# One chunk first, modulation chunks moved back, and a norm's residual scaling spread out

## The chip, the cores and the metric

The kernel runs on one core of one Trainium2 chip. The metric is the device time of one execution in microseconds (us); the kernel before took 3770.34 us (median of three runs, 3767.11 to 3773.52).

## The reference, cut to what matters

A first block of two layers (each: feed-forward, token mixer, feed-forward, all with modulation and a post-norm) is followed by a second block of two layers with RMS norms. The change touches the first block only. Activations are 512 tokens by 1024 features.

```python
cond = silu(c)
for l in range(2):
    mod = cond @ w_ada[l] + b_ada[l]                 # 1024 x 9216, then split into nine parts of 1024
    sh1, sc1, g1, sh2, sc2, g2, sh3, sc3, g3 = split(mod, 9)
    y = swiglu(x * (1 + sc1) + sh1, w_gate, w_up, w_down)     # 1024 -> 2816 -> 1024
    x = layer_norm(ALPHA * x + 0.5 * (1 + g1) * y)
    y = token_mixer(x * (1 + sc2) + sh2, w_in, w_out)
    x = layer_norm(ALPHA * x + (1 + g2) * y)
    y = swiglu(x * (1 + sc3) + sh3, ...)
    x = layer_norm(ALPHA * x + 0.5 * (1 + g3) * y)
```

## The kernel before, in words

**Layout.** Everything is transposed: a tile is 128 features by 512 tokens, and the residual XR is eight such tiles (`NT` = 8). Products are taken in three matmuls on a high and a low part of both operands (`mul3`: high by high, high by low, low by high). HH and HL are the two parts of a stage's input h, WH and WL those of a weight chunk, AH and AL those of the feed-forward's hidden tiles.

**Weight stream.** Weights come in chunks of 256 output columns (128 x 2048 floats, 1 MB). SyncE issues each as one DMA into one of three staging buffers (STAGE, `NS` = 3), in the order in which the plan takes the chunks. `split` lets ScalarE copy a chunk into one of two WH buffers (`NW` = 2) once the chunk that held the buffer is done, and `low` lets VectorE subtract to get WL; TensorE waits for that ("w.lo"). A staging buffer is free for the chunk three places on when WL is there. `take` gives out the next chunk, and splits the one after it first; `ahead`, called inside a norm, does that a little earlier for the second chunk of the coming stage, but only if the place right behind the first chunk in the stream is a weight chunk: a raw chunk there makes it return nothing.

**Modulation.** The matrix w_ada has 72 chunks. Eight are done at the start; the other 64 are raw chunks, strung into the same stream. `take` adds `rate` (0.62) to `due` for most chunks, and when `due` reaches 1 it calls `ada`, which puts one modulation chunk right behind the chunk just taken: nine VectorE operations (`ada_rows`, L1892 to L1898). After every second one, `ada_flush` follows two releases later: TensorE sums over partitions (`ada_sum`, eight matmul instructions) and VectorE adds the bias. `modded` flushes at once if a pending pair holds values that the caller needs. `ffn` calls it for its gate through `gate`, right after the first tile of the first down chunk.

**Start of a stage.** `ffn` and `first_mixer` begin with `pair`: three dummy matmuls (`keep`), then for the first chunk the products with h tiles 0 to 2 (18 matmuls), the same for the second chunk, then tile 3 of both, then the rest of the first and the rest of the second: 96 matmuls. `pair` is there because h comes tile by tile. In the stream it takes the chunk `self.taken`, so a modulation chunk between the two is simply passed.

**Norm.** `layer_norm` plans `ln_a` (mean, subtraction, squares, variance), `ln_b` (scale, and h tile by tile on VectorE, ScalarE and GpSimd) and `ln_x`, eight ScalarE operations on the residual (L1627), which are planned right behind h and ahead of the next stage's first `take`.

**Background.** `tick` is called after each few matmuls in the plan and advances the generators in `self.active` by one step each; attention units are run that way. Each engine's program is the plan's steps in order; engines meet at semaphores only.

Of the kernel before, what the change touches and what calls it, by code (L numbers as in the profile page):

```python
# [22 lines left out]
ACT = mybir.ActivationFunctionType  # L23
# [5 lines left out]
NT = D // P  # L29
# [9 lines left out]
FFN_GROUPS = [(0, 8), (8, 8), (16, 6)]  # L39
ODD_ORDER = (4, 5, 0, 6, 1, 7, 2, 3)  # L40
MLP_GROUPS = [(0, 8), (8, 8), (16, 8), (24, 8)]
# [57 lines left out]
class Plan:  # L99
# [241 lines left out]
    def layer_norm(self, l, idx, total, nxt):  # L341
        sid, acc = total
        if nxt:
            self.modded(nxt[0], nxt[2])
            self.modded(nxt[0], nxt[1])
        s, mean = self.small.take(), self.banks.take()
        self.tmp.free(acc[0], ("ln.mean", sid))
        sq = []
        for n in range(NT):
            sq.append(self.tmp.take())  # L350
            if n in (1, 3, 5):
                self.tmp.free(sq[n - 1], ("ln.fold", sid, n))
        self.tmp.free(sq[6], ("ln.fold", sid, 7))
        var = self.held.take()
        low = self.ahead()
        self.add("ln_a", l, idx, sid, acc[0], nxt, list(self.xv), s, mean, sq, var, low)
        self.banks.free(mean, ("ln.sub", sid, NT - 1))
        for n in (1, 3, 5, 7):
            self.tmp.free(sq[n], ("ln.var", sid, n))
        y, rs = self.yr.take(), self.banks.take()  # L360
        self.held.free(var, ("rs.v", sid))
        if nxt:
            self.hv += 1
            self.add("ln_b", sid, y, var, rs, s, self.hfree, self.hv, self.to_h(), low)
            self.banks.free(rs, ("ln.sc", sid, NT - 1))
            self.add("ln_x", sid, s, self.hv, [v + 1 for v in self.xv])
            self.xv = [v + 1 for v in self.xv]
            self.small.free(s, ("x", NT - 1, self.xv[NT - 1]))
            self.yr.free(y, ("ln.rs", sid))
            return None  # L370
        sq = []
        for n in range(NT):
            sq.append(self.tmp.take())
            if n in (1, 2, 3, 5):
                self.tmp.free(sq[n - 1], ("ll.fold", sid, n))
        self.tmp.free(sq[6], ("ll.fold", sid, 7))
        self.xv = [v + 1 for v in self.xv]
        self.add("ln_last", l, idx, sid, y, var, rs, sq, list(self.xv), low)
        self.banks.free(rs, ("ll.x", sid, NT - 1))
        self.yr.free(y, ("ln.rs", sid))  # L380
        self.small.free(s, ("ln.sub", sid, NT - 1))
        return [(sq[n], ("ll.fold", sid, n)) for n in (3, 5, 7)]

    def rms_norm(self, name, l, total, meanwhile=None):
        rid, low = self.new(), None
# [18 lines left out]
            meanwhile[1]()  # L404


    def ffn(self, kind, st, names, l, groups, gate, mean):
        total = (self.new(), [])
        afree = [None, None]
        for gi, (g0, G) in enumerate(groups):  # L410
            self.av += 1
            av, a = self.av, gi % 2
            for mi in range(G // 2):
                idx, first = l * names["n_up"] + g0 // 2 + mi, gi == 0 and mi == 0
                qs = []
                ch = self.take(names["gate" if kind == "swiglu" else "up"], idx)
                for t, (b, pid) in enumerate(self.pair(ch, "h", self.hv) if first else self.feat2(ch, 8, "h", self.hv)):
                    q = self.tmp.take()
                    self.add("act", kind, pid, b, q)
                    self.banks.free(b, ("act", pid))  # L420
                    if kind == "swiglu":
                        qs.append((q, pid))
                    else:
                        self.add("a_part", av, a, 2 * mi + t, q, ("act.sq", pid), afree[a])
                        self.tmp.free(q, ("a.lo", av, 2 * mi + t))
                self.release(ch, ("proj", pid))
                if kind == "swiglu":
                    ch = self.take(names["up"], idx)
                    for t, (b, pid) in enumerate(self.feat2(ch, 8, "h", self.hv)):
                        q, gid = qs[t]  # L430
                        self.add("glu", pid, gid, b, q)
                        self.banks.free(b, ("glu", pid))
                        self.add("a_part", av, a, 2 * mi + t, q, ("glu", pid), afree[a])
                        self.tmp.free(q, ("a.lo", av, 2 * mi + t))
                    self.release(ch, ("proj", pid))
            if gi == len(groups) - 1:
                self.hfree = ("proj", pid)
            done, s = [], None
            for c in range(4):
                ch = self.take(names["down"][gi], l * 4 + c, ada=gi < len(groups) - 1 or c == 0)  # L440
                for t in range(2):
                    b, pid = self.feat(ch, G, 256, t, "a%d" % a, av)
                    if gate and not gate[-1]:
                        gate[-1] = self.gate(l, gate[0], 0.5)
                    self.upd(2 * c + t, b, pid, gate[-1] if gate else None)
                    done.append(2 * c + t)
                self.release(ch, ("proj", pid))
                afree[a] = ("proj", pid)
                if gi == len(groups) - 1 and mean:
                    self.total(mean, *total, done[:-2] if c < 3 else done)  # L450
                    done = done[-2:] if c < 3 else []
        if gate:
            self.small.free(gate[-1][0], ("x", NT - 1, self.xv[NT - 1]))
        return total if mean != "rms" else self.squares(*total)
# [41 lines left out]
    def first_mixer(self, l):  # L496
        hv = self.hv
# [2 lines left out]
        nk_done, sb_done, out_done = {}, [], {}  # L500

        def proj(idx, key, paired=False):
            ch = self.take("w_in", l * 12 + idx)
            for t, (b, pid) in enumerate(self.pair(ch, "h", hv) if paired else self.feat2(ch, 8, "h", hv)):
                self.add("m_copy", l, key, t, pid, b)
                self.banks.free(b, ("m.p", l, key, t))
            self.release(ch, ("proj", pid))
# [129 lines left out]
        for c in range(2):  # L637
            ch = self.take("w_in", l * 12 + 4 + c)
# [16 lines left out]
        gate = self.gate(l, 5, 1.0)  # L655
# [482 lines left out]
    def whole(self):  # L1138
        self.ada_first()
        self.fill = [(0, c) for c in range(8, 36)] + [(1, c) for c in range(36)]  # L1140
        self.modulate_first()
        ffn1 = {"gate": "ffn1_w_gate", "up": "ffn1_w_up", "down": ["ffn1_down0", "ffn1_down1", "ffn1_down2"], "n_up": 11}
        ffn2 = {"gate": "ffn2_w_gate", "up": "ffn2_w_up", "down": ["ffn2_down0", "ffn2_down1", "ffn2_down2"], "n_up": 11}
        for l in range(2):
            self.rate = 0.62
            total = self.ffn("swiglu", "f1%d" % l, ffn1, l, FFN_GROUPS, [2, None], "ln")
            self.layer_norm(l, 0, total, (l, 3, 4))
            total = self.first_mixer(l)
            self.layer_norm(l, 1, total, (l, 6, 7))
            if l == 1:  # L1150
                self.add("c2_load", self.hv)
                self.bg.append(self.rope_tables())
            total = self.ffn("swiglu", "f2%d" % l, ffn2, l, FFN_GROUPS, [8, None], "ln")
            total = self.layer_norm(l, 2, total, (1, 0, 1) if l == 0 else None)
        assert not self.fill
        self.pipeline()
        mlp = {"up": "w_up", "down": ["down_m0", "down_m1", "down_m2", "down_m3"], "n_up": 16}
        for l in range(2):
            self.rms_norm("g_mix", l, total)
            if l == 0:  # L1160
                self.even_mixer()
            else:
                self.odd_mixer()
            total = self.cross(l, ("w_out_e", "w_out_o")[l])
            self.rms_norm("g_mlp", l, total)
            total = self.ffn("relu2", "mlp%d" % l, mlp, l, MLP_GROUPS, None, "rms" if l == 0 else None)
        self.add("store", list(self.xv))


# [397 lines left out]
def scalar(e, m, plan):  # L1567
# [52 lines left out]
                act.activation(m.HH[:, n, :], m.XR[:, n, :], ACT.Identity, bias=B[:, n:n + 1], scale=A[:, n:n + 1]).then_inc(  # L1620
                    *e.up("act_hh", "h.hi", hv, n))

    def ln_x(sid, s, hv, xv):
        AG, AB = m.small(s)[:, 16:24], m.small(s)[:, 24:32]
        for n in range(NT):
            e.wait_ge(("h.hi", hv, n), ("h.q", hv, n))
            act.activation(m.XR[:, n, :], m.XR[:, n, :], ACT.Identity, bias=AB[:, n:n + 1], scale=AG[:, n:n + 1]).then_inc(  # L1627
                *e.up("act_x", "x", n, xv[n]))

    def ln_last(l, idx, sid, y, var, rs, sq, xv, low_of):  # L1630
        beta = m.vec("ln_bias", l * 24 + idx * 8, 8)
# [1273 lines left out]
```

## Time and profile before

| | |
|---|---|
| median of the timed runs | 3770.34 us (3767.11 to 3773.52) |
| profiled execution, its own time | 3772.04 us |
| its span in the trace | 3770.7 us |
| TensorE matmuls | 3610.5 us busy, 96% of the span |
| VectorE / ScalarE / GpSimd | 1765.6 / 1234.9 / 497.4 us |
| chain that ended last | 85% matmuls of L1236 |

The matmul line of nearly all projections is L1236, so a tile's name tells them apart: `s_hh,s_wh` is h by a chunk's high part, `s_cc` alone is a dummy matmul, `s_cc,s_tmp` with one column is a sum over partitions. A row of the timeline has start, length, engine, line, operation, and in brackets how long the engine had been idle and what it waited for. Matmuls overlap, so the distance of two starts is the rate, not the length of one.

### The profile page before, as it was taken

To read this page: it belongs to the slowest core of one execution; us is meant where nothing else is said; L and a number is where in the kernel's file an instruction comes from. 1 tells how busy PE (TensorE), PEld (TensorE's weight loads), DVE (VectorE), ACT (ScalarE), POOL (GpSimd) and SP (SyncE) were. 2 spreads that over 40 slices of the span, in tenths; PEclk is the share of its full clock that TensorE was granted. 3 is DMA by queue.
4 is the path that set the end of the run, shared out by engine and by line. 5 is a ranking of instruction groups with operands and counts; after the bars stand their busy time and mean duration, and the time that the engine had idled before them with its cause. 6 is when DMAs were issued, how large, how long until landed. Compare 5 with 4: busy or idle time off the path is not lost.

```text
span 3770.7 us, 41104 instructions
## 1 busy us (share of the span) xinstructions
PE 3610.5 (96%) x16878; PEld 2921.0 (77%) x16878; DVE 1765.6 (47%) x3091; ACT 1234.9 (33%) x1670; POOL 497.4 (13%) x433
## 2 busy tenths in 40 slices
PE   8999999999998999999999999988999999999999
PEld 7888867688886888867788877746878887787888
DVE  4444553554545444444532244785553334554332
ACT  2222361342223222462332223335442223343222
POOL 0010110110011010121110010111121111202111
PEclk9999999999998999999999998978999999999999
DMA  6444222134442434211122221101212222222222
GB/s 243 159 147 152 104 90 90 56 123 145 158 144 82 164 145 145 90 45 45 56 99 92 98 84 56 57 12 34 90 67 90 101 101 81 90 79 78 101 92 76
DMA packets 52605, 373.42 MB, mean 99 GB/s; under 512 B 5825, under 2 KB 5953, under 8 KB 9538
## 3 DMA queue, kind: packets, MB, share of 16 engines
q1 hardware_dynamic: 52418, 370.79, 27.4%
q8 instruction: 133, 2.18, 0.2%
q14 instruction: 54, 0.44, 0.0%
HBM read 368.67 MB, written 2.10 MB: 98 GB/s over the span
## 4 chain that ended last, share of the span: by engine, by line
PE 85%; DVE 8%; ACT 4%; issue 2%; POOL 1%; DMA 0%; DVEq 0%; ACTq 0%; SPq 0%; POOLq 0%
PE ps L1236 85%; DVE s_wl L1879 1%; ACT s_wh L1571 1%; PE ps L1261 0%; DVE s_tmp L2109 0%; ACT L1676 0%; ACT s_tmp L1707 0%; DVE s_hl L1872 0%; DVE s_tmp L2099 0%; POOL s_tmp L2385 0%; DVE s_xr L1959 0%; ACT s_hh L1571 0%; DVE s_tmp L2015 0%; DVE s_sm L2107 0%; DVE s_na L1862 0%
## 5 line engine op out<-in xcount | busy, mean ns | idle before, releaser
L1236 PE MATMUL ps<-s_hh,s_wh 128*128 128x512 f32 (+1 forms) x2840 | 1133.2, 399 | 56.3 <-DVE s_wl L1879 31.5
L1236 PE MATMUL ps<-s_hl,s_wh 128*128 128x512 f32 (+1 forms) x2840 | 1115.0, 393 | 0.0
L1236 PE MATMUL ps<-s_hh,s_wl 128*128 128x512 f32 (+1 forms) x2840 | 1113.6, 392 | 0.0
L1879 DVE TENSOR_TENSOR s_wl<-s_stage,s_wh 128x2048 fp32r<-128x2048 f32 (+3 forms) x296 | 634.7, 2146 | 744.5 <-ACT s_wh L1571 744.4
L1571 ACT ACTIVATE s_wh<-s_stage 128x2048 fp32r<-128x2048 f32 (+1 forms) x277 | 519.9, 1877 | 771.6 <-PE ps L1236 661.1
L1236 PEld LDWEIGHTS ps<-s_hh,s_wh 128*128 128x128 f32 (+1 forms) x2840 | 538.3, 190 | 202.0 <-issue 41.4
L1236 PEld LDWEIGHTS ps<-s_hh,s_wl 128*128 128x128 f32 (+1 forms) x2840 | 537.5, 189 | 115.6
L1236 PEld LDWEIGHTS ps<-s_hl,s_wh 128*128 128x128 f32 (+1 forms) x2840 | 538.3, 190 | 111.3 <-issue 2.2
L1236 PE MATMUL ps<-s_ah,s_wh 128*128 128x512 f32 x1216 | 475.6, 391 | 0.0
L1236 PE MATMUL ps<-s_ah,s_wl 128*128 128x512 f32 x1216 | 474.3, 390 | 0.0
L1236 PE MATMUL ps<-s_al,s_wh 128*128 128x512 f32 x1216 | 474.1, 390 | 0.0
L2405 POOL TENSOR_TENSOR s_al<-s_tmp,s_ah 128x512 fp32r<-128x512 f32 x152 | 196.4, 1294 | 1749.2 <-ACT s_ah L1571 1749.2
L1236 PEld LDWEIGHTS ps<-s_ah,s_wl 128*128 128x128 f32 x1216 | 228.7, 188 | 47.8
L1236 PEld LDWEIGHTS ps<-s_al,s_wh 128*128 128x128 f32 x1216 | 228.9, 188 | 47.0
L1236 PEld LDWEIGHTS ps<-s_ah,s_wh 128*128 128x128 f32 x1216 | 228.8, 188 | 47.1
L1595 ACT ACTIVATE s_tmp<-ps 128x512 f32<-128x512 f32 x152 | 90.8, 597 | 498.4 <-PE ps L1236 498.1
L1571 ACT ACTIVATE s_ah<-s_tmp 128x512 fp32r<-128x512 f32 x152 | 96.0, 632 | 417.1 <-DVE s_tmp L2030 361.9
L1930 DVE SCALAR_TENSOR_TENSOR s_xr<-ps,s_sm,s_xr 128x512 f32<-128x512 f32 x112 | 83.6, 749 | 225.1 <-PE ps L1236 224.5
L1932 DVE TENSOR_TENSOR s_xr<-ps,s_xr 128x512 f32<-128x512 f32 x96 | 66.2, 690 | 232.6 <-PE ps L1236 232.6
L1895 DVE SCALAR_TENSOR_TENSOR s_tmp<-s_stage,s_cond,s_tmp 128x256 f32<-128x256 f32 x366 | 150.8, 478 | 0.0
L2030 DVE TENSOR_TENSOR s_tmp<-s_tmp,ps 128x512 f32<-128x512 f32 x88 | 60.2, 686 | 168.5 <-PE ps L1236 168.3
L1236 PEld LDWEIGHTS ps<-s_cc,s_tmp 128*128 128x128 f32 x852 | 115.2, 209 | 22.2 <-POOL s_tmp L2396 6.7
(416 smaller groups left out, 3445.5 us busy)
## 6 DMA issues: line engine op xcount, KB each, us to landing
s_stage<-in_w_ada SPq DMA_DIRECT2D x64, 1024.0 KB, 4.8
s_stage<-in_ffn_w_gate SPq DMA_DIRECT2D x44, 1024.0 KB, 4.8
s_stage<-in_ffn_w_up SPq DMA_DIRECT2D x44, 1024.0 KB, 4.8
s_stage<-in_ffn_down SPq DMA_DIRECT2D x32, 1024.0 KB, 4.8
s_stage<-in_w_up SPq DMA_DIRECT2D x32, 1024.0 KB, 4.7
s_stage<-in_down_m SPq DMA_DIRECT2D x32, 1024.0 KB, 4.8
s_stage<-in_w_in SPq DMA_DIRECT2D x24, 1024.0 KB, 4.8
s_stage<-in_ffn_down SPq DMA_DIRECT2D x16, 768.0 KB, 4.2
```

Source lines behind the costliest of these rows:

```text
L1236: return pe.matmul(out, lhs, rhs, start=start, stop=stop, skip_group_check=True)
L1571: return act.activation(out, src, ACT.Copy)
L1595: act.activation(m.tmp(q), m.bank(b), ACT.Silu if kind == "swiglu" else ACT.Relu).then_inc(*e.up("act_ffn", "act", pid))
L1879: ins = dve.tensor_tensor(m.WL[:, ws, a:z], m.STAGE[:, j % NS, a:z], m.WH[:, ws, a:z].bitcast(F32), ALU.subtract)
L1895: ins = dve.scalar_tensor_tensor(dst, w[:, k, :], cond, dst, ALU.mult, ALU.add)
L1930: ins = dve.scalar_tensor_tensor(x, m.bank(b), m.small(gate[0])[:, n:n + 1], x, ALU.mult, ALU.add)
L1932: ins = dve.tensor_tensor(x, m.bank(b), x, ALU.add)
L2030: dve.tensor_tensor(m.tmp(q), m.tmp(q), m.bank(b), ALU.mult).then_inc(*e.up("dve_ffn", "glu", pid))
L2405: pool.tensor_tensor(m.AL[a][:, k, :], m.tmp(q), m.AH[a][:, k, :].bitcast(F32), ALU.subtract).then_inc(*e.up("pool_a", "a.lo", av, k))
```

## The change

The first feed-forward of layer 0 no longer begins with `pair`; its first chunk runs alone, both tiles in step with h, without dummy matmuls. The first chunk (mixer) or the first two (feed-forward) of a stage no longer add to `due`. `rate` is 0.64 in place of 0.62. `ln_x` does one tile per call, and the calls are made by a generator that `tick` advances: two ticks do nothing, then one tile per tick. An argument of `ffn` that nothing used is gone.

```diff
@@ layer_norm
-            self.add("ln_x", sid, s, self.hv, [v + 1 for v in self.xv])
             self.xv = [v + 1 for v in self.xv]
-            self.small.free(s, ("x", NT - 1, self.xv[NT - 1]))
+            self.active.append(self.scaled(sid, s, self.hv, list(self.xv)))
...
+    def scaled(self, sid, s, hv, xv):
+        yield
+        for n in range(NT):
+            yield
+            self.add("ln_x", sid, s, hv, n, xv[n])
+        self.small.free(s, ("x", NT - 1, xv[NT - 1]))
@@ ffn
-    def ffn(self, kind, st, names, l, groups, gate, mean):
+    def ffn(self, kind, names, l, groups, gate, mean, paired=True):
...
-                ch = self.take(names["gate" if kind == "swiglu" else "up"], idx)
-                for t, (b, pid) in enumerate(self.pair(ch, "h", self.hv) if first else self.feat2(ch, 8, "h", self.hv)):
+                ch = self.take(names["gate" if kind == "swiglu" else "up"], idx, ada=not first)
+                both = first and paired
+                tiles = self.pair(ch, "h", self.hv) if both else self.feat2(ch, 8, "h", self.hv, first)
+                for t, (b, pid) in enumerate(tiles):
...
-                    ch = self.take(names["up"], idx)
+                    ch = self.take(names["up"], idx, ada=not first)
@@ first_mixer, proj
-            ch = self.take("w_in", l * 12 + idx)
+            ch = self.take("w_in", l * 12 + idx, ada=not paired)
@@ whole
-            self.rate = 0.62
-            total = self.ffn("swiglu", "f1%d" % l, ffn1, l, FFN_GROUPS, [2, None], "ln")
+            self.rate = 0.64
+            total = self.ffn("swiglu", ffn1, l, FFN_GROUPS, [2, None], "ln", l > 0)
@@ scalar
-    def ln_x(sid, s, hv, xv):
+    def ln_x(sid, s, hv, n, v):
         AG, AB = m.small(s)[:, 16:24], m.small(s)[:, 24:32]
-        for n in range(NT):
-            e.wait_ge(("h.hi", hv, n), ("h.q", hv, n))
-            act.activation(m.XR[:, n, :], ...).then_inc(*e.up("act_x", "x", n, xv[n]))
+        e.wait_ge(("h.hi", hv, n), ("h.q", hv, n))
+        act.activation(m.XR[:, n, :], ...).then_inc(*e.up("act_x", "x", n, v))
```

## Rows read from the trace of the kernel before

**Rows 1.** The page, part 1: busy time, share of the span, instructions.
```profile
PE 3610.5 (96%) x16878; PEld 2921.0 (77%) x16878; DVE 1765.6 (47%) x3091; ACT 1234.9 (33%) x1670; POOL 497.4 (13%) x433
```

**Rows 2.** Waits of TensorE: who waited for whom, total us, times, longest.
```profile
PE ps L1236 <- DVE s_wl L1879: 33.9, 7, 13.9
```

**Rows 3.** The chain that ended last, in time: start, length, what.
```profile
54.20 369.26 PE ps L1236 x1644
...
1173.52 2.30 DVE s_wl L1879
1175.86 368.27 PE ps L1236 x1644
```

**Rows 4.** Timeline of TensorE, the first feed-forward's start.
```profile
39.83 2.93 PE L1236 MATMUL ps<-s_cc 128*128 128x256 f32 x6 [2.45 <-DVE s_wl L1879]
42.20 0.99 PE L1236 MATMUL ps<-s_hh,s_wh 128*128 128x512 f32 x1
54.20 0.79 PE L1236 MATMUL ps<-s_hh,s_wh 128*128 128x512 f32 x1 [7.06 <-DVE s_wl L1879]
60.28 0.40 PE L1236 MATMUL ps<-s_hh,s_wl 128*128 128x512 f32 x1
74.84 0.39 PE L1236 MATMUL ps<-s_hh,s_wh 128*128 128x512 f32 x1
```

**Rows 5.** Windows: bounds, length, matmul busy (count), granted clock, DMA share, GB/s.
```profile
54.20:60.21 6.01, 6.01 (x14) 0.50 0.50 174
```

**Rows 6.** Timeline of ScalarE and VectorE in the same stretch.
```profile
49.92 1.89 ACT L1571 ACTIVATE s_wh<-s_stage 128x2048 fp32r<-128x2048 f32 x1
49.46 0.69 DVE L1872 TENSOR_TENSOR s_hl<-s_tmp,s_hh 128x512 fp32r<-128x512 f32 x1
51.85 2.29 DVE L1879 TENSOR_TENSOR s_wl<-s_stage,s_wh 128x2048 fp32r<-128x2048 f32 x1 [1.70 <-ACT s_wh L1571]
```

**Rows 7.** Windows around a TensorE pause of 4.81 us that ended at 3170.29.
```profile
3166.30:3169.75 3.45, 0.00 (x0) 1.00 0.00 0
3169.75:3173.17 3.42, 2.88 (x7) 0.50 0.55 172
```

**Rows 8.** Timeline of the stage start at 1156 us: TensorE, then ScalarE.
```profile
1156.52 0.51 PE L1236 MATMUL ps<-s_hh,s_wh 128*128 128x512 f32 x1 [0.24 <-DVE s_hl L1872]
1195.30 0.39 PE L1236 MATMUL ps<-s_hh,s_wl 128*128 128x512 f32 x1
1165.95 5.73 ACT L1627 ACTIVATE s_xr<-s_xr,s_sm 128x512 f32<-128x512 f32 x8
1189.60 1.28 ACT L1595 ACTIVATE s_tmp<-ps 128x512 f32<-128x512 f32 x2 [16.12 <-PE ps L1236]
```

**Rows 9.** Timeline of TensorE, first and 96th matmul of the stage at 1558 us.
```profile
1558.70 0.50 PE L1236 MATMUL ps<-s_hh,s_wh 128*128 128x512 f32 x1
1581.38 0.39 PE L1236 MATMUL ps<-s_hh,s_wl 128*128 128x512 f32 x1
```

**Rows 10.** Timeline of TensorE, VectorE and GpSimd at the first down chunk.
```profile
141.08 0.95 PE L1236 MATMUL ps<-s_cc,s_tmp 128*128 128x1 f32 x8
149.70 0.42 DVE L1898 TENSOR_TENSOR s_tmp<-s_tmp 128x256 f32<-128x256 f32 x1
142.71 1.30 POOL L2405 TENSOR_TENSOR s_al<-s_tmp,s_ah 128x512 fp32r<-128x512 f32 x1 [4.16 <-ACT s_ah L1571]
```

**Rows 11.** Timeline of VectorE: modulation chunk and attention step in mixer 0; a chunk's low part in mixer 1.
```profile
496.71 0.42 DVE L1898 TENSOR_TENSOR s_tmp<-s_tmp 128x256 f32<-128x256 f32 x1
497.05 0.74 DVE L2053 TENSOR_TENSOR s_tmp<-s_tmp,ps 128x256 f32<-128x256 f32 x2
...
1584.24 2.29 DVE L1879 TENSOR_TENSOR s_wl<-s_stage,s_wh 128x2048 fp32r<-128x2048 f32 x1 [3.15 <-ACT s_wh L1571]
```

**Rows 12.** Windows: both mixers, from first h matmul to the next stage's.
```profile
439.75:769.35 329.60, 309.10 (x1566) 0.95 0.21 77
1558.70:1874.75 316.05, 301.26 (x1535) 0.96 0.15 54
```

More of the change, by code:

```diff
@@ L1152, in whole @@
                 self.bg.append(self.rope_tables())
-            total = self.ffn("swiglu", "f2%d" % l, ffn2, l, FFN_GROUPS, [8, None], "ln")
+            total = self.ffn("swiglu", ffn2, l, FFN_GROUPS, [8, None], "ln")
             total = self.layer_norm(l, 2, total, (1, 0, 1) if l == 0 else None)
@@ L1165, in whole @@
             self.rms_norm("g_mlp", l, total)
-            total = self.ffn("relu2", "mlp%d" % l, mlp, l, MLP_GROUPS, None, "rms" if l == 0 else None)
+            total = self.ffn("relu2", mlp, l, MLP_GROUPS, None, "rms" if l == 0 else None)
         self.add("store", list(self.xv))
@@ L1621, in ln_b @@
                     *e.up("act_hh", "h.hi", hv, n))
-    def ln_x(sid, s, hv, xv):
+    def ln_x(sid, s, hv, n, v):
         AG, AB = m.small(s)[:, 16:24], m.small(s)[:, 24:32]
-        for n in range(NT):
-            e.wait_ge(("h.hi", hv, n), ("h.q", hv, n))
-            act.activation(m.XR[:, n, :], m.XR[:, n, :], ACT.Identity, bias=AB[:, n:n + 1], scale=AG[:, n:n + 1]).then_inc(
-                *e.up("act_x", "x", n, xv[n]))
+        e.wait_ge(("h.hi", hv, n), ("h.q", hv, n))
+        act.activation(m.XR[:, n, :], m.XR[:, n, :], ACT.Identity, bias=AB[:, n:n + 1], scale=AG[:, n:n + 1]).then_inc(
+            *e.up("act_x", "x", n, v))
     def ln_last(l, idx, sid, y, var, rs, sq, xv, low_of):
```

## The prediction

> **What bounds the kernel now.** I read the page's busy table first: TensorE's matmuls fill 96% of the span, and VectorE, the next engine, less than half [rows 1]. So time can come only from stretches in which TensorE stands still or runs slowly. TensorE's waits name the largest of them: VectorE's low part of a weight chunk (L1879), 33.9 us in 7 waits, one of 13.9 us [rows 2]. The chain in order of time shows where: a feed-forward is a run of 368 us or so with nothing else in it, and the run that starts at 1175.86 comes directly after a low part at 1173.52 [rows 3]. Inside feed-forwards nothing waits; at their starts something does. The timeline gives the two places: a 7.06 us wait that ends at 54.20 [rows 4] and the 13.9 us one. The granted clock adds a second price, for after the 7.06 us wait TensorE has 0.50 of its clock (1.2 GHz) for 6.01 us [rows 5]. Fourteen matmuls take 60.28 - 54.20 = 6.08 us there, 0.434 us each, and the next 64 take 74.84 - 60.28 = 14.56 us, 0.2275 each [rows 4].
>
> **Part 1, the first feed-forward begins with one chunk.** Before: 18 matmuls from 42.20, then the wait for the second chunk's low part (ScalarE's copy at 49.92, VectorE's 2.29 us to 54.14 [rows 6]), then the other 78 of the pair's 96, so that the third chunk begins at 74.84 [rows 4]. Now the first chunk has all 48 of its matmuls to do before it needs the second. Tile 7 of h is ready at 50.15 [rows 6], tiles come about 1.2 us apart and six matmuls take 6 x 0.2275 = 1.37, so h does not hold them up. The plan still puts the second chunk's copy behind the same sixteen ScalarE operations, so 54.14 stays.
> The three dummy matmuls go too (six instructions, 39.83 to 42.76 [rows 4]). They were hidden, as TensorE had nothing else to do, but they had TensorE streaming when h came. Without them it has done only one-column sums and then paused. I take it to begin at 0.50: if low for t us, it falls back by t/2. t is between the 3.4 us of the short low stretch in [rows 7] and the 6.0 us of [rows 5]; I take 4.5, nearer to the start's own 39.83 to about 43, where it rose. 96 matmuls from 42.20 then end at 42.20 + 96 x 0.2275 + 2.25 = 66.3. The second chunk is asked for at 42.20 + 10.92 + 2.25 = 55.4, after 54.14, so there is no wait. Gain 74.84 - 66.3 = **8.5 us** (bounds 7.8 and 9.1).
> The rule that speaks against this edit is in the Trainium skill (TensorE: Matmul & The Clock Gate, section "What's actually happening"): the throttled clock is the default and activity releases it, so leaving out warming work means a cold start. No row shows this start without the dummies. By that rule the sum stands as above. If the clock were up within a microsecond as before, the first chunk would end near 53.5, wait for 54.14, and the gain would be about 9.7.
> The third chunk needs the first one's buffer: free at 55.4, then two evictions of 0.64 each [rows 8], a copy of 1.9 and a low part of 2.3 [rows 6] make it ready at about 60.9, before 66.3.
>
> **Part 2, no modulation chunk among the first two.** I counted `due` through the whole plan. With 0.62 a modulation chunk comes in a stage's first two only once, at the second layer's first feed-forward, between gate and up. There `ahead` finds a raw chunk and returns nothing; the up chunk's copy then stands behind the eight ScalarE operations of L1627 (1165.95, 5.73 us [rows 8]). First matmul to 96th is 1195.30 - 1156.52 = 38.78 us [rows 8]. At the stage start at 1558.70, where `ahead` works, it is 1581.38 - 1558.70 = 22.68 [rows 9]; the three other stages with the pair's second chunk ready also take 22.7. The norm ahead is no longer for it. Gain 38.78 - 22.68 = **16.1 us**; this contains the slow clock after the wait. It has a near-exact twin, so I give it only 1 us either way.
> The same count moves the others. In the first feed-forward modulation chunks 8, 9, 10 now stand behind up 1, up 2 and gate 3, and chunk 11, which stood behind gate 3, now stands behind the **first down chunk**. The gate needs exactly chunks 8 to 11 and is planned after that chunk's first tile: the flush puts a sum on TensorE that waits for chunk 11's nine VectorE operations. This is a wait that was not there. Its price: chunk 12 stands in that place now and ends at 149.70 + 0.42 = 150.12. The sum before it at 141.08 goes, so the first tile's 24 matmuls run from 141.08 to 146.54 (the last hidden tile, at 144.01, is in time [rows 10]), and TensorE stands until 150.2: 3.7 us. The sum itself is only moved. Behind it are queued the down chunk's second tile on TensorE and, on VectorE, the bias, the gate, both residual updates and the next low part, which has a chunk's length in hand. To this comes the clock: after a pause of 4.81 us it was at 0.50 for 3.42 us, 2.88 of them busy, 1.44 lost [rows 7]. I take 1.4: **+5.1 us** (bounds 0, if chunk 11 is done early, and 3.7 + 3.0, if the clock is low for the 6.0 us of [rows 5]).
>
> **Part 3, rate and the mixers.** The number of modulation chunks is 64 as before. Mixer 0 keeps eight, two of them moved by one or two chunks; mixer 1 gets its first, chunk 71, behind its second weight chunk. There VectorE is idle 3.15 us after one low part [rows 11], and one chunk takes some 3.4, so nearly all is hidden; the sum of its pair on TensorE (0.95 us [rows 10]) moves there from a feed-forward and is no gain or loss. A modulation chunk between a low part and an attention step's subtraction, as that ending at 497.05 [rows 11], does delay the step by its 3.4 us. With eight of them mixer 0 takes 329.60 against 316.05, 13.55 or 1.7 each [rows 12]. I take +0.5 for the one more (bounds -2, if one leaves the chain of steps, and +3.4).
>
> **Part 4, the residual's scaling spread out.** Forty operations as before, none added; only their place on ScalarE changes: four ahead of the first chunk's evictions, four behind. Ahead of the first eviction ScalarE is idle 16.12 us [rows 8], which hides all eight either way, and their first reader is the residual update at the stage's end. **0**; if that cover were gone, 5.73 us at each of five norms. Where it did matter, at 1166, part 2 already counts it.
>
> **Sum.** -8.5 - 16.1 + 5.1 + 0.5 = -19.0 us. On the profiled execution: 3772.04 - 19.0 = 3753.0. That execution is 1.7 above the median of 3770.34, so I forecast **3751.3 us**.
>
> **Rivals.** *The new sum does not wait* (TensorE is slower to it, or chunk 11 is done by then): -24.1, 3746. For it: bounds of zero; against: the same VectorE order at 149.70 now. *The start gains nothing*, because h or the cold clock stretches the first chunk, or the third chunk comes late: -10.5, 3760. *The wait at 1162 stays in part*: the up chunk's copy is freed of the 5.73 us but is not made ahead: -8.5 - 5.7 + 5.6 = -8.6, 3762. *The order is not what I counted* and both waits stay: within 0.2%, 3770. **Slower**: the spread operations stand ahead of something TensorE waits for. In five norms 8 x 0.72 = 5.73 us each is 28.7; with -19.0 it gives +9.7, 3780. It turns the sign once over 19.0 / 5 = 3.8 us per norm is exposed, and against it stand the idle 16.12 us, and that ScalarE is busy for 33% only [rows 1].
>
> **How the numbers follow.** Forecast 0.55, no wait 0.15, start gains nothing 0.11, wait stays in part 0.09, order not as counted 0.04, slower 0.06. Bounds of the parts around the forecast: 3745 to 3757. To leave out no more than two in ten, and since three runs of the kernel before already spread over 6 us, the range is 3744 to 3760. Changes under 0.2% (7.5 us) cannot be told from none; all cases but the last two are beyond that, though the two small ones only just: faster 0.90, same 0.05, slower 0.05.
>
> **What would show it.** In the changed profile: 48 matmuls without a wait from about 42, the first ones 0.43 us apart, and the third chunk begun near 66; no L1879 wait near 1145, and 22.7 us from first to 96th matmul there; a new TensorE wait of 3 to 4 us for a sum near 138 us, behind the first 24 matmuls on hidden tiles; the mixers within 2 us of 329.6 and 316; L1627 in single operations. Wrong would be a wait for L1879 in either start, more than 3 us more in mixer 1, or ScalarE named by TensorE's waits after a norm.

## The result, and the profile after

Times in us: median, lowest and highest of the single runs.

| | before | changed |
|---|---|---|
| median | 3770.52 (12 runs) | 3761.68 (12 runs, 3758.06 to 3771.74) |
| ratio | | 0.9981, 95% interval 0.9972 to 0.999 |
| profiled execution, its span | 3772.04, 3770.7 | 3758.06, 3756.7 |
| mean granted clock in it | 0.966 | 0.969 |

The ratio is not the quotient of the medians: it lies near that of the means (3762.95 and 3770.12), and so reads 7.2 us where the medians differ by 8.8. The same holds for the tables below.

By the medians the changed kernel is 8.8 us faster where I had forecast 19.0, and 3761.7 lies outside my range of 3744 to 3760. The profiled executions alone differ by 14.0: that of before lay 1.5 above its median, that of the changed kernel 3.6 below its own. So 5.0 of the missing 10.2 can be looked for in the profile, and the other 5.1 or so are these two distances.

The busy table of the changed kernel, to be laid beside [rows 1]:
```profile
PE 3609.8 (96%) x16872; PEld 2917.7 (78%) x16872; DVE 1765.9 (47%) x3093; ACT 1235.4 (33%) x1670; POOL 497.4 (13%) x433
```
Six dummy matmuls are gone, and TensorE's busy time is within 0.7 us of before. The gain is in its waits (who waited for whom, total, times, longest; L1887 is the low part, L1906 the end of a modulation chunk, L2425 the rope product on GpSimd):
```profile
PE ps L1245 <- DVE s_wl L1887: 11.2, 6, 4.8
PE ps L1245 <- POOL s_nk L2425: 10.4, 6, 4.1
```
Against [rows 2] the wait for low parts fell from 33.9 to 11.2 us. The second line, which the text below calls the wait for the rope product, rose from 7.7 us in 6 waits, the longest 3.5 (in the kernel before it is `PE ps L1236 <- POOL s_nk L2417`).

**The start.** TensorE's timeline there, beside [rows 4]:
```profile
42.07 0.77 PE L1245 MATMUL ps<-s_hh,s_wh 128*128 128x512 f32 x1 [4.82 <-POOL s_hl L2369]
42.64 0.63 PE L1245 MATMUL ps<-s_hl,s_wh 128*128 128x512 f32 x1
...
46.90 0.44 PE L1245 MATMUL ps<-s_hh,s_wl 128*128 128x512 f32 x1
...
66.27 0.39 PE L1245 MATMUL ps<-s_hh,s_wh 128*128 128x512 f32 x1
```
The first matmuls are 0.43 us apart and last 0.63, until about 46.9; from there on they are 0.2275 apart and last 0.39. The third chunk begins at 66.27 (74.84 before), and no wait for a low part stands between. The windows view (bounds, length, busy time and count of matmuls, weight loads, VectorE, ScalarE and GpSimd, then granted clock, DMA share, GB/s) reads a granted clock of 1.00 from 42.07 to 46.90, so its records miss this stretch, and only the spacing and length of the matmuls show that the engine was at the lower of its two levels (1.2 GHz):
```profile
42.07:46.90 4.83, 4.83 (x11) 3.77 (x12) 4.83 (x7) 4.83 (x8) 3.20 (x2) 1.00 0.51 213
```
The Trainium skill (TensorE: Matmul & The Clock Gate, section "What's actually happening") has the throttled clock as the default that activity releases; the trace agrees, with 4.8 us in which matmuls start half as often as behind it.

**The norm at 1158**, beside [rows 8], TensorE and then ScalarE:
```profile
1158.18 0.79 PE L1245 MATMUL ps<-s_hh,s_wh 128*128 128x512 f32 x1
1180.89 0.39 PE L1245 MATMUL ps<-s_hh,s_wl 128*128 128x512 f32 x1
```
```profile
1167.62 2.92 ACT L1635 ACTIVATE s_xr<-s_xr,s_sm 128x512 f32<-128x512 f32 x4
1175.20 1.28 ACT L1604 ACTIVATE s_tmp<-ps 128x512 f32<-128x512 f32 x2 [4.66 <-PE ps L1245]
```
First to 96th matmul is 22.71 us in place of 38.78. Four of the eight scalings (L1635) now stand ahead of the first eviction, the rest behind it; TensorE names none of them.

**The gate's sum.** TensorE at the first down chunk, beside [rows 10], and the windows around the new wait, with the columns as above:
```profile
141.64 1.02 PE L1245 MATMUL ps<-s_cc,s_tmp 128*128 128x1 f32 x8 [3.54 <-DVE s_tmp L1906]
```
```profile
138.10:141.64 3.54, 0.00 (x0) 0.03 (x1) 3.41 (x10) 0.00 (x0) 0.00 (x0) 1.00 0.64 222
141.64:146.00 4.36, 4.36 (x16) 3.67 (x17) 1.09 (x3) 0.00 (x0) 0.00 (x0) 0.61 0.77 301
```
TensorE has nothing for 3.54 us while VectorE works through the nine operations of modulation chunk 11, and then has matmuls 0.43 us apart, half clock, until about 146.0. From the first down chunk's first matmul to that of the next chunk on h it takes 49.81 us in place of 44.61, that is +5.20.

**The mixers**, beside [rows 12], with the columns as above:
```profile
436.34:771.37 335.03, 312.94 (x1566) 237.69 (x1567) 166.72 (x334) 139.62 (x218) 50.75 (x58) 0.94 0.21 76
1545.92:1861.39 315.47, 300.73 (x1543) 229.34 (x1543) 143.09 (x268) 139.59 (x218) 50.72 (x58) 0.97 0.16 57
```
Mixer 0 takes 5.4 us more, mixer 1 takes 0.6 less. The stretches of the program add up to the difference of -14.0. The start, up to the first down chunk, has -9.3: 8.4 of them come before the third chunk, and 0.8 is a modulation sum that no longer stands there. The gate has +5.2. Mixer 0 with its norm and the next feed-forward up to its first down chunk has +4.5. The norm at 1158, counted up to the next down chunk, has -16.2, and the norm ahead of mixer 1 +1.6. The rest moves by 1 us or less each.

### The profile page after: what moved, and what is told of

The parts are those of the page before. It is cut to its first block, busy times and chain, and to the rows that moved or that the text cites. A ratio compares the mean times of both kernels' runs of the same rounds, so it can differ in the third digit from the quotient of the medians.

```text
span 3756.7 us, 41109 instructions
## 1 busy us (share of the span) xinstructions
PE 3609.8 (96%) x16872; PEld 2917.7 (78%) x16872; DVE 1765.9 (47%) x3093; ACT 1235.4 (33%) x1670; POOL 497.4 (13%) x433
## 4 chain that ended last, share of the span: by engine, by line
PE 86%; DVE 7%; ACT 4%; issue 2%; POOL 1%; DMA 0%; DVEq 0%; SPq 0%; ACTq 0%; POOLq 0%
PE ps L1245 86%; DVE s_wl L1887 1%; ACT s_wh L1580 1%; PE ps L1270 0%; ACT L1684 0%; POOL s_tmp L2393 0%; DVE s_tmp L2117 0%; ACT s_tmp L1715 0%; DVE s_tmp L2107 0%; DVE s_tmp L2023 0%; DVE s_hl L1880 0%; ACT s_hh L1580 0%; DVE s_tmp L1903 0%; POOL s_hl L2369 0%; DVE s_sm L2115 0%
## 5 line engine op out<-in xcount | busy, mean ns | idle before, releaser
L1887 DVE TENSOR_TENSOR s_wl<-s_stage,s_wh 128x2048 fp32r<-128x2048 f32 (+3 forms) x298 | 634.5, 2132 | 704.1 <-ACT s_wh L1580 704.0
L2034 DVE TENSOR_TENSOR s_tmp<-s_tmp 128x512 f32<-128x512 f32 x64 | 47.1, 736 | 166.7 <-ACT s_tmp L1604 166.5
```

Of the source, the lines that this page charges most:

```text
L1887: ins = dve.tensor_tensor(m.WL[:, ws, a:z], m.STAGE[:, j % NS, a:z], m.WH[:, ws, a:z].bitcast(F32), ALU.subtract)
L2034: dve.tensor_tensor(m.tmp(q), m.tmp(q), m.tmp(q), ALU.mult).then_inc(*e.up("dve_ffn", "act.sq", pid))
```

## The experiments

Here "the chunks' order" is the list of weight chunks behind which the plan puts a modulation chunk. In most of these kernels it is written out, as a set AT of indices (counted from 0 over the whole program), and the rate no longer matters:

```
-        self.due += self.rate if ada else 0
-        if self.due >= 1:
-            self.due -= 1
+        self.taken_w += 1
+        if self.taken_w - 1 in AT:
             ...
```
The kernel before ran again beside each four of them: its median was 3770.44 for e1 to e4, 3770.33 for e5 to e8 and 3772.08 for e9 to e12. Differences are of medians, against that value.

### The changed kernel once more, and its three parts alone

e1 is the changed kernel unchanged. e2 has the start alone:
```
-  def ffn(self, kind, st, names, l, groups, gate, mean):
+  def ffn(self, kind, st, names, l, groups, gate, mean, paired=True):
...
-  self.pair(ch, "h", self.hv) if first else self.feat2(ch, 8, "h", self.hv)
+  self.pair(ch, "h", self.hv) if first and paired else self.feat2(ch, 8, "h", self.hv, first)
...
-  total = self.ffn("swiglu", "f1%d" % l, ffn1, l, FFN_GROUPS, [2, None], "ln")
+  total = self.ffn("swiglu", "f1%d" % l, ffn1, l, FFN_GROUPS, [2, None], "ln", l > 0)
```
e3 has the order alone:
```
-  ch = self.take(names["up"], idx)            (and the same for gate)
+  ch = self.take(names["up"], idx, ada=not first)
...
-  ch = self.take("w_in", l * 12 + idx)
+  ch = self.take("w_in", l * 12 + idx, ada=not paired)
...
-  self.rate = 0.62
+  self.rate = 0.64
```
e4 has the scaling alone:
```
-  self.add("ln_x", sid, s, self.hv, [v + 1 for v in self.xv])
+  self.active.append(self.scaled(sid, s, self.hv, list(self.xv)))
...                                             (`scaled` and `ln_x` as in the change)
```

> The changed kernel once more. Its first profile is 14.0 us shorter than the profile of before, its median 8.8. Theory A (the schedule made mixer 0 longer): the profile again shows 334 to 336 us from mixer 0's first h matmul to the next stage's, against 329.6 before, and the 3.5 us wait for the modulation sum at the first down chunk; the gains at the start (8.5) and at the layer 1 norm (16.2) are there too. Theory B (chance of the clock): mixer 0 comes out within 1.5 us of 329.6 in this profile, because its low stretches fall elsewhere. Both expect a spread of single times of more than 6 us.

> The kernel before with only the first feed-forward begun by one chunk; modulation chunks and the residual's scaling as before. All theories: TensorE's 7.06 us wait gone, the third chunk begun 8.5 us earlier, no wait for a modulation sum near 141, the norm at 1156 still with its 13.9 us wait. 8.5 us shorter than before (7.8 to 9.1 by the clock's start), 3762. If leaving out the dummy matmuls costs more than I took, 4 to 6 us shorter only.

> The kernel before with only the modulation chunks moved (none among a feed-forward's first two, rate 0.64); the pair and the scaling as before. Theory A1 (the moved modulation chunks lengthen mixer 0): -16.1 at the norm, +5.1 for the sum at the first down chunk, +5 in mixer 0: 6 us shorter, 3764.5, and mixer 0 at 334 to 336. Theory A2 (the spread scaling lengthens it) and B (clock): 11 us shorter, 3759.5, mixer 0 within 1.5 us of 329.6.

> The kernel before with only the residual's scaling spread out. Theory A2 (ScalarE's spread operations stand in mixer 0's attention steps): mixer 0 at 334 to 336, but at the layer 1 norm the up chunk's copy no longer stands behind 5.7 us of them, so in sum about 1 us shorter, 3769. Theory A1 and B: mixer 0 unchanged, and up to 5.7 us saved at that norm: 3765. My prediction's part 4 said 0 with the order changed.

| | median (runs) | ratio, 95% interval | difference |
|---|---|---|---|
| e1, changed again | 3759.25 (8) | 0.9975, 0.9965 to 0.9984 | -11.2 |
| e2, start alone | 3762.45 (9) | 0.9982, 0.9972 to 0.9992 | -8.0 |
| e3, order alone | 3771.01 (12) | 1.0003, 0.9995 to 1.0011 | +0.6 |
| e4, scaling alone | 3769.76 (11) | 0.9998, 0.999 to 1.0007 | -0.7 |

The three add up to -8.1, and the changed kernel has -8.8 or -11.2. So by the medians the start gives all of the gain, and the order, from which I had expected -10.5 (-16.1 + 5.1 + 0.5), gives nothing, although its profile shows the norm's gain in full (from the norm's first matmul to the next down projection 89.97 us, 106.19 before) and the gate's +5.2. Something else in the order must cost about what the forecast is short of. e4 shows by the way that the spread scaling alone frees the up chunk's copy (that same stretch is 4.7 us shorter), but its median does not tell this from no change.

e1's profile, which spans 3756.0 us, repeats the start, the gate's +5.2 and the norm at 1158. In the mixers it differs: mixer 0 takes 330.99 us, 1.4 more than before where the first profile had 5.4, and mixer 1 takes 319.87, 3.8 more where the first had 0.6 less. So one profile's +5.4 is in part chance. Most of the difference between the two lies in one stretch of mixer 0, with the same 108 matmul records in both, first in the changed kernel's first profile and then in e1's:
```profile
676.54:696.40 19.86, 18.42 (x108) 13.02 (x109) 11.18 (x41) 7.24 (x22) 0.00 (x0) 0.78 0.00 1
676.20:692.10 15.90, 14.46 (x108) 10.32 (x109) 11.04 (x42) 7.25 (x22) 0.00 (x0) 1.00 0.01 2
```
The same program had a granted clock of 0.78 there once and of 1.00 the other time, and that is 4.0 us.

### The order taken apart

e5 changes one index of before's order (the norm's), e6 gives mixer 0 the changed kernel's order, e7 moves one modulation chunk into mixer 1, and e8 is the changed kernel with the gate's last modulation chunk one weight chunk earlier:
```
e5, of before's order:         84 -> 85
e6, of before's order:         36 -> 37, 44 -> 45, 24 -> 53
e7, of before's order:         112 -> 119
e8, of the changed kernel's:   8 -> 7
```

> The kernel before with one modulation chunk moved by one place: chunk 54 stands behind the layer 1 up chunk in place of between gate and up; all 63 others where they were. Theory C (what the new order takes back is lost where the other chunks now stand, in the mixers and at the first gate): 16 us shorter, 3754, since nothing else moves. Theory D (the norm's gain is given back by itself, as low clock in the stages behind it): 0 to 8 us shorter.

> The kernel before with mixer 0's eight modulation chunks placed and paired as in the changed kernel (one goes from behind w_in 11 to behind w_in 0, one from behind w_in 7 to behind w_in 8, and one chunk of the first feed-forward goes to the second so that the pairs end where they do there); the rest as before. Theory C1 (mixer 0's new places cost): 4 to 5 us longer, 3775. Theory C2 (only mixer 1's chunk costs) and the clock's chance: within 1.5 us of before.

> The kernel before with the last modulation chunk moved from the layer 1 feed-forward into mixer 1, behind its second weight chunk, as in the changed kernel; the rest as before. Theory C2: 3 to 4 us longer, 3774 (mixer 1 with its norm 409.9 in place of 406). My prediction: within 0.5 us, as VectorE is idle there and the pair's sum only moves.

> The changed kernel with modulation chunk 11 one place earlier, behind up 3 in place of behind the first down chunk; all others as there. The sum that the first gate needs then has its rows long before: the 3.5 us wait and the 3.4 us of low clock behind it go. 5.1 us shorter than the changed kernel by my prediction's term, about 3756; if the pause is only moved, no shorter than it.

| | median (runs) | ratio, 95% interval | difference |
|---|---|---|---|
| e5, norm's chunk moved | 3756.11 (5) | 0.9965, 0.9951 to 0.9979 | -14.2 |
| e6, mixer 0 as changed | 3778.22 (11) | 1.0019, 1.001 to 1.0028 | +7.9 |
| e7, one into mixer 1 | 3772.44 (11) | 1.0005, 0.9996 to 1.0014 | +2.1 |
| e8, changed, gate mended | 3753.16 (5) | 0.9955, 0.9941 to 0.9968 | -17.2 |

The norm's gain is real: one number changed in the order brings -14.2. The gate's price is real too: e8 is 6.1 faster than e1 and 8.5 faster than the changed kernel's first runs, and the wait is gone. TensorE in e8:
```profile
137.20 0.39 PE L1247 MATMUL ps<-s_ah,s_wl 128*128 128x512 f32 x1
137.43 0.95 PE L1247 MATMUL ps<-s_cc,s_tmp 128*128 128x1 f32 x8
138.23 0.49 PE L1247 MATMUL ps<-s_ah,s_wh 128*128 128x512 f32 x1
```
The sum follows the matmul before it at once and the clock stays up (1.00 from 137.43 to 142.00); the stretch takes 44.48 us again. What the forecast had at next to nothing is mixer 0: +7.9 in e6 (by the ratio's interval 3.8 to 10.6). Mixer 1's +2.1 cannot be told from no change, and the profiles do not settle it: mixer 1 took 315.5 to 319.9 us in the five kernels with a chunk in it (three times 319.8 or 319.9) and 314.4 to 318.9 in the nine without. With -14.2, +7.9, +2.1 and +6.1 to +8.5 the order comes to +2 to +4, and e3 measured +0.6 (its interval is -1.9 to +4.1). Each term has an uncertainty of some 3 us, so this agreement says little.

### Why mixer 0 costs: the pairs or the places

Two modulation chunks share one sum on TensorE. e6 changed two things in mixer 0: where two of its eight modulation chunks stand, and, as one was taken out ahead of it, which of them end a pair and so carry a sum. In mixer 0 e9 changes the second alone:
```
e9, of before's order:         24 -> 53
```

> The kernel before with one modulation chunk of the first feed-forward moved to the second: mixer 0 keeps its eight in their old places, but the pairs end one chunk earlier or later, so the sums stand elsewhere on TensorE. e6, which moved two chunks as well, took 7.9 us more. Theory P (the sum's place: the one that stood at 97.6 us of the mixer, where TensorE waits anyway, is gone from there): 4 to 8 us longer, with the 4 us step between the mixer's 385th and 457th projection matmul. Theory Q (the nine VectorE operations' place): within 1.5 us of before, no step.

e9: median 3778.00 (12 runs), ratio 1.0015, interval 1.0005 to 1.0025, +5.9 us. So the pairs alone cost, and what the places add (2.0 between the medians of e6 and e9) cannot be told from nothing. A part of both numbers belongs to the edit and not to mixer 0: `24 -> 53` puts five modulation chunks in a row into the feed-forward behind it, and there TensorE waits 0.42 and 0.90 us for low parts in e9, and 0.41 and 0.77 in e6. The changed kernel, whose order has at most two in a row there, does not wait.

Where mixer 0's own cost sits can be seen by laying the projections' matmuls of mixer 0 side by side. In the six kernels with the changed pairs (the changed kernel, e1, e3, e6, e8, e9) the stretch from the 385th to the 457th lasts 3.8 to 4.9 us longer than before; in the six with the old ones (e2, e4, e5, e7, e10, e12) it is within 0.01 us of before. That stretch in the kernel before, TensorE and then VectorE:
```profile
537.30 0.95 PE L1236 MATMUL ps<-s_cc,s_tmp 128*128 128x1 f32 x8
539.77 0.36 PE L1236 MATMUL ps<-s_wh,s_hh 128*128 128x256 f32 x1 [1.51 <-ACT s_rv L1571]
...
553.66 2.87 PE L1236 MATMUL ps<-s_nk,s_cc 128*128 128x384 f32 x12 [1.54 <-POOL s_nk L2417]
```
```profile
541.47 2.29 DVE L1879 TENSOR_TENSOR s_wl<-s_stage,s_wh 128x2048 fp32r<-128x2048 f32 x1 [0.86 <-ACT s_wh L1571]
...
546.70 0.43 DVE L1898 TENSOR_TENSOR s_xm<-s_xm,s_tmp 128x256 f32<-128x256 f32 x1
547.04 0.74 DVE L2053 TENSOR_TENSOR s_xm<-s_xm,ps 128x256 f32<-128x256 f32 x2
551.97 0.56 DVE L2045 SCALAR_TENSOR_TENSOR s_nk<-ps,s_tmp 128x384 f32<-128x384 f32 x1 [4.18 <-ACT s_tmp L1676]
```
And in e9:
```profile
548.83 5.25 PE L1238 MATMUL ps<-s_nk,s_cc 128*128 128x384 f32 x12 [4.08 <-POOL s_nk L2419]
```
```profile
536.63 2.29 DVE L1881 TENSOR_TENSOR s_wl<-s_stage,s_wh 128x2048 fp32r<-128x2048 f32 x1 [0.92 <-ACT s_wh L1573]
...
541.86 0.42 DVE L1900 TENSOR_TENSOR s_tmp<-s_tmp 128x256 f32<-128x256 f32 x1
542.21 0.74 DVE L2055 TENSOR_TENSOR s_xm<-s_xm,ps 128x256 f32<-128x256 f32 x2
547.14 0.56 DVE L2047 SCALAR_TENSOR_TENSOR s_nk<-ps,s_tmp 128x384 f32<-128x384 f32 x1 [4.19 <-ACT s_tmp L1678]
```
VectorE's chain is the same in both: low part, the nine operations of a modulation chunk, the attention step's subtraction, and the result that GpSimd takes 10.5 us after the low part began. What differs is how much TensorE has to do beside it. Before, its sum (0.95 us) and a wait of 1.51 stood there, so it came to the rope product late and waited 1.54 more. In e9 these 2.5 us are gone from that place, 48 projections run through, and TensorE comes 2.5 us earlier to a product that is not: it waits 4.08. Behind that longer wait the clock is down, and the twelve matmuls take 5.25 us in place of 2.87 (the windows view reads 1.00 in the kernel before and 0.54 in e9):
```profile
553.66:556.53 2.87, 2.87 (x14) 2.12 (x14) 1.07 (x2) 0.99 (x2) 0.49 (x2) 1.00 0.00 0
548.83:554.08 5.25, 5.25 (x14) 3.56 (x14) 1.07 (x2) 0.99 (x2) 0.82 (x2) 0.54 0.00 0
```
2.5 of wait and 2.4 of clock are the 4.9 of the step. But the 2.5 of wait are no loss: they are the 0.95 and 1.51 us that stood just ahead of the 385th matmul before and are gone from there. Counted from the 337th matmul, which takes both in, the stretch to the 457th lasts 28.45 or 28.46 us with the old pairs and 29.83 to 30.83 with the changed ones. So the net price of this place is 1.4 to 2.4 us, and it is the clock's. The changed kernel has the same wait, with 1.55 of clock behind it:
```profile
552.39 4.42 PE L1245 MATMUL ps<-s_nk,s_cc 128*128 128x384 f32 x12 [4.08 <-POOL s_nk L2425]
```
The sums themselves only move: a stretch that gains one is 0.8 to 1.0 us longer, and one that loses one is as much shorter.

Much stays open. The place and its mechanism explain 1.4 to 2.4 us, and the waits behind mixer 0 another 1.2 to 1.3 in e6 and e9; the medians have +5.9 and +7.9. The profiles cannot show the rest. Mixer 0 took 328.6 to 335.1 us in the six with the changed pairs (median 331.5) and 326.3 to 332.4 in before and the six with the old ones (median 329.6). One stretch further on, from the 673rd to the 769th projection (it holds the one shown above for e1), took 60.8 to 67.9 in the first group and 61.8 to 68.0 in the second. e9's own profile, at 3770.68 us, lies 7.3 below the median of e9, and its mixer 0 (328.64) is even shorter than before.

### The parts put together

e10 is the changed kernel with before's order but for the one index (84 -> 85): the start, the spread scaling and the norm's gain, without the gate's wait and with mixer 0's old pairs. e11 goes further and takes all eight modulation chunks out of mixer 0, into feed-forwards:
```
e11, of e10's order:   35, 36, 38, 40, 41, 43, 44, 46 out, and 8;
                       7, 10, 15, 21, 26, 28, 90, 98, 106 in
```
e12 is e10 with the three dummy matmuls of before kept at the start (`mm2` puts them ahead of the chunk's first matmul):
```
-  yield from self.rest_of(*self.begin(ch, kt, n, x, ver, order), 0)
+  yield from self.rest_of(*self.begin(ch, kt, n, x, ver, order), 0, 3 if self.av == 1 else 0)
...
```

> The changed kernel with the modulation chunks placed as in the kernel before, but for chunk 54, which stands behind the layer 1 up chunk. It has the start (measured 8.0), the norm (14.2) and the spread scaling (0.7), and none of what the other moves cost: 23 us shorter than before, 3747.5. If gains at two places don't add, at least 14.

> As e10, but mixer 0's eight modulation chunks go into the first and third feed-forward (24 behind the first one's 34 chunks), so that no mixer has any. Mixer 0 took 13.5 us more than mixer 1, which had none; four sums of 0.95 us only move. Theory (VectorE's operations and sums in the attention steps are what they cost): 9 us shorter than e10, 3738. Rival (staging: with 24 raw chunks in one feed-forward the weight chunks land late): new waits for L1879's like in the first feed-forward, and no shorter than e10.

> As e10, with the three dummy matmuls back ahead of the first chunk. In the changed kernel the first eleven matmuls ran 0.43 us apart until 46.9. With the dummies the clock is up near 43 and the first chunk ends near 53.3, but the second is ready at 54.1 only: 1.2 us shorter than e10 at most, by the profile; in the medians no difference that can be told.

| | median (runs) | ratio, 95% interval | difference |
|---|---|---|---|
| e10, good parts | 3751.49 (5) | 0.9951, 0.9938 to 0.9964 | -20.6 |
| e11, mixers free as well | 3742.44 (5) | 0.9924, 0.9912 to 0.9936 | -29.6 |
| e12, e10 with dummies | 3748.02 (5) | 0.9938, 0.9926 to 0.995 | -24.1 |

The start, the norm and the scaling measured alone give -8.0 - 14.2 - 0.7 = -22.9, and e10 has -20.6: the parts add up once the order costs nothing elsewhere. e11 is the fastest of all, and its profile shows where, first the window of mixer 0 and then TensorE's wait for the rope product in it:
```profile
431.32:743.30 311.98, 297.93 (x1535) 226.90 (x1535) 139.81 (x258) 139.66 (x218) 50.84 (x58) 0.97 0.15 55
```
```profile
PE ps L1247 <- POOL s_nk L2427: 1.8, 3, 0.9
```
Mixer 0 without modulation takes 311.98 us, 4.1 less than mixer 1 in [rows 12]; in the kernel before it took 329.60 and in e10 329.74, in the kernel before with 5.9 us of this wait in place of 1.8. Four sums (32 matmuls) are gone from it, and its clock rose from 0.95 to 0.97. The rival, that 24 modulation chunks in the first feed-forward make weight chunks late, did not come true: TensorE has no wait for a low part between 42 and 430 us. Mixer 0 is 17.8 us shorter than in e10; the two profiles differ by 14.3 in all, as the feed-forwards now hold the eight chunks and their sums, and the medians by 9.0. e12 is 3.5 below e10, but the intervals overlap; in the two profiles its first 96 matmuls on h take 22.82 us against 23.43. So leaving out the dummies costs 0.6 us in the profile; whether it costs more in the medians is not settled.

## Why the prediction was wrong, step by step

- **Part 1, the start, -8.5 (bounds 7.8 to 9.1): right.** e2 measured -8.0 by its medians (-6.8 by its ratio). The third chunk begins at 66.27, where I had 66.3, and the low clock lasted 4.8 us, where I took 4.5 from between [rows 5] and [rows 7].
- **Part 2, the norm, -16.1: right.** 38.78 became 22.71 (forecast 22.68). One index alone gives -14.2 in e5; its interval, -7.9 to -18.5, holds the -16.1.
- **Part 2, the gate's sum, +5.1: right in the profile, perhaps low in the medians.** The last matmul and the sum start 3.93 us apart in place of 0.23, which is the 3.7 of the forecast (3.54 of it shown as a wait), and 1.5 of clock make it +5.20. Mending it gave 6.1 to 8.5.
- **Part 3, rate and mixers, +0.5 (bounds -2 and +3.4): the step that failed.** e6 measured +7.9 for mixer 0 with its new places and pairs, e9 +5.9 for its pairs alone (of each, 1.2 to 1.3 us of waits belong to the edit), and e7 +2.1 (not told from nothing) for mixer 1. The prediction saw that two of mixer 0's chunks move, priced what a chunk does to VectorE, and said of the sum that goes to mixer 1 that its move "is no gain or loss". It did not follow that dropping one modulation chunk ahead of mixer 0 shifts every pair in it (19 stood ahead of it, now 18). A sum had filled TensorE's time ahead of a result that was late anyway; with the sum elsewhere the wait for that result grows from 1.54 to 4.08 us, and 1.4 to 2.4 us of low clock follow. The bounds were made from VectorE's side only, so they could not hold this. That this step failed is shown by e6 and e9, and e10, which among other things takes mixer 0's old pairs back, agrees; what makes up the rest of their +5.9 to +7.9 is open.
- **Part 4, the scaling, 0: right.** e4 measured -0.7. In a kernel with the old order it frees the up chunk's copy (-4.7 in that stretch); with the new order there is nothing left for it to free.
- **Sum.** With +7.9 and +2.1 in place of +0.5 the same sum gives -8.5 - 16.1 + 5.1 + 10.0 = -9.5, against -8.8 and -11.2 measured. The two new terms are uncertain by some 3 us each, so that it comes so near is partly luck.
- **The range.** It reached to 3760 by rivals that touched the start and the norm. The rival with the number 3762 (the wait at 1162 stays in part) met the measured 3761.7, but by luck: that wait is gone. The lower bound of 3745 is a slip as well, for the parts' bounds add up to 3742 to 3757.5. No rival put a loss in a mixer; my slower case was the spread scaling, of which e4 shows no cost.
- **What was to be seen.** Of the marks named ahead, four were met (half spacing at the start, third chunk near 66, 22.7 us at the norm, a 3 to 4 us wait near 138); "the mixers within 2 us" was not: the first profile has +5.4 in mixer 0, and e1's +1.4 there but +3.8 in mixer 1. The last is also more than the 3 us in mixer 1 that I had called a sign of being wrong.

## What to carry to other kernels

When a fixed share of side work is spread over a plan by a counter, a change of the rate moves every item behind the first: list the new places of all of them, and of what follows in pairs or groups, before pricing any. Price each item by what its engine waits for next. A small operation ahead of a late result is free, and taking it away only lengthens the wait; here the longer wait then brought the clock down, so that taking work away cost 1.4 to 2.4 us. Where a stage has a chain of small dependent steps, side work belongs in a stage without one (e11: 9 us for eight chunks).

## What the runs showed that I had not expected

- Single runs of one kernel spread over more than the effects looked for: before ran from 3765.68 to 3780.92 us in the 17 runs beside e9, and e9 from 3770.35 to 3788.07. The spans go with the mean granted clock (of those 17, the fastest spans 3764.4 us at 0.969 and the slowest 3779.6 at 0.963). So one profile cannot price an edit of less than about 10 us in this kernel; that figure is my estimate from these spreads. The stretch from mixer 0's first matmul to the next down chunk alone took 416.4 to 422.5 us in the seven profiles with before's order there.
- A longer wait can cost more than itself. Waits of 1.54 to 1.56 us leave the next twelve matmuls at 2.87 us; waits of 4.07 to 4.08, at the same place, leave them at 4.26 to 5.25 us.
- A step between two matmuls of the same number can mislead. The 3.8 to 4.9 us from the 385th on hold 2.5 us that had stood just ahead of it.
